# Two kinds of projection in pairs of units: 512 weight columns per matmul

## The reference

```python
def parallel_mixer(h, ...):
    proj = h @ w_in
    lx, ly, fq, fk, fv, ff, rq, rk, rv, rg = jnp.split(proj, ...)   # 256 256 512 512 512 8 256 256 256 256
    lru_out = rg_lru(causal_depthwise_conv(lx, ...), ...) * jax.nn.gelu(ly)
    fox_out = forgetting_attention(fq, fk, fv, ff, fox_b_f)         # 8 heads of 64
    ret_out = retention(rq, rk, rv, rg, positions)                  # 4 heads of 64, rotary on rq and rk
    return jnp.concatenate([lru_out, fox_out, ret_out], axis=-1) @ w_out

def memory_cross_attention(h, mem_n, w_q, w_k, w_v, w_o):
    ...
    v = (mem_n @ w_v).reshape(bsz, m, CROSS_HEADS, CROSS_HEAD_DIM)
    ...
```

## Time and profile before

| | us |
|---|---|
| median of 3 runs | 2244.64 (2243.01 to 2245.59) |
| profiled execution | 2244.02 |
| its span | 2242.2 |
| PE busy | 1789.8 (80%) |
| DVE busy | 842.8 (38%) |
| ACT busy | 551.4 (25%) |

### The profile page before, as it was taken

How to read it: one execution, slowest core, us unless ns; L and a number is a source line. 1 busy time by engine, 2 the same in 40 slices (tenths; PEclk the granted TensorE clock), 3 DMA queues, 4 the chain that set the end, 5 groups by cost and what they waited for, 6 DMA issues and landing times.

```text
span 2242.2 us, 27619 instructions
## 1 busy us (share of the span) xinstructions
PE 1789.8 (80%) x11942; PEld 1119.9 (50%) x11942; DVE 842.8 (38%) x1328; ACT 551.4 (25%) x841; POOL 88.0 (4%) x136
## 2 busy tenths in 40 slices
PE   8999999999999999998666666665666666576666
PEld 7899888899888888864112111221111211121111
DVE  5755788867678887741100100110010010010101
ACT  5745544456545444630000000000000000000000
POOL 1200000012100000000000000000000000000000
PEclk9999999999999999999878877887887887888788
DMA  8345667754547675599999999999999999999997
GB/s 265 130 157 194 196 226 250 239 172 143 197 150 234 228 262 168 226 426 429 430 429 430 429 430 429 429 430 430 428 430 429 430 430 430 430 429 430 429 430 315
DMA packets 172217, 739.73 MB, mean 330 GB/s; under 512 B 6800, under 2 KB 133264, under 8 KB 147008
## 3 DMA queue, kind: packets, MB, share of 16 engines
q1 hardware_dynamic: 169744, 731.27, 81.8%
q0 software_dynamic: 2352, 6.69, 0.9%
HBM read 736.88 MB, written 1.05 MB: 329 GB/s over the span
## 4 chain that ended last, share of the span: by engine, by line
DMA 49%; PE 41%; DVE 5%; ACT 2%; issue 1%; POOL 0%; SPq 0%; DVEq 0%; POOLq 0%; ACTq 0%
PE PS L399 40%; DMA WB<-in_w_up 24%; DMA WB<-in_w_down 24%; DVE WL L1853 1%; DMA W<-in_w_in 1%; ACT WH L1278 1%; DVE S L1848 1%; DVE X L1848 1%; PE PS L558 0%; POOL T L2742 0%; DVE CN L1845 0%; DVE S L1845 0%; PE PS L687 0%; DVE S L1962 0%; PE PS L532 0%
## 5 line engine op out<-in xcount | busy, mean ns | idle before, releaser
L399 PE MATMUL PS<-WB,XS 128*32 128x352 f32 x3520 | 405.7, 621 | 238.5 <-DMA WB<-in_w_up 163.1
L399 PE MATMUL PS<-HT,WH 128*128 128x256 f32 (+1 forms) x1456 | 383.9, 338 | 4.7 <-DVE WL L1853 2.4
L399 PEld LDWEIGHTS PS<-WB,XS 128*32 128x32 f32 x3520 | 130.2, 138 | 508.4 <-DMA WB<-in_w_up 218.7
L1853 DVE TENSOR_TENSOR WL<-W,WH 128x2048 fp32r<-128x2048 f32 x135 | 310.2, 2298 | 132.6 <-ACT WH L1278 132.5
L1278 ACT ACTIVATE WH<-W 128x2048 fp32r<-128x2048 f32 x141 | 270.0, 1915 | 244.4 <-PE PS L399 242.2
L399 PE MATMUL PS<-WB,S 128*32 128x512 f32 x1054 | 221.8, 773 | 118.5 <-DMA WB<-in_w_down 92.3
L1848 DVE SCALAR_TENSOR_TENSOR S<-S,PS 128x352 f32<-128x352 f32 (+1 forms) x66 | 33.3, 525 | 717.6 <-PE PS L399 402.4
L399 PE MATMUL PS<-HT,WL 128*128 128x256 f32 x1064 | 296.7, 282 | 0.0
L399 PEld LDWEIGHTS PS<-HT,WH 128*128 128x128 f32 x1456 | 249.7, 191 | 36.7 <-DVE WL L1853 3.6
L399 PE MATMUL PS<-WH,MX 128*128 128x512 f32 x672 | 216.2, 394 | 1.3 <-DVE MX L2333 0.9
L399 PEld LDWEIGHTS PS<-HT,WL 128*128 128x128 f32 x1064 | 203.3, 191 | 0.8
(11 more groups left out here) (281 smaller groups left out, 1879.1 us busy)
## 6 DMA issues: line engine op xcount, KB each, us to landing
WB<-in_w_up SPq DMA_DIRECT2D x63, 2816.0 KB, 36.3
WB<-in_w_gate SPq DMA_DIRECT2D x47, 2816.0 KB, 35.2
WB<-in_w_down SPq DMA_DIRECT2D x46, 2816.0 KB, 35.9
CN<-in_w_gate SPq DMA_DIRECT2D x16, 2816.0 KB, 36.5
CN<-in_w_down SPq DMA_DIRECT2D x15, 2816.0 KB, 36.1
W<-in_w_in SPq DMA_DIRECT2D x31, 1024.0 KB, 5.4
S<-in_w_ada SPq DMA_DIRECT2D x24, 1024.0 KB, 5.3
W<-in_w_gate SPq DMA_DIRECT2D x22, 1024.0 KB, 7.8
```

The source lines that it names most:

```text
L399: return e.matmul(o, l, r, start=start, stop=stop, skip_group_check=True)
L1853: e.tensor_tensor(M.WL[i][:, :], M.SLOT[m % NW], M.WH[i][:, :].bitcast(F32), ALU.subtract).then_inc(*up("low", m))
```

## The change

The units of v, of rq with rk, and of rv with rg in the mixer, and those of w_cv, no longer hold 256 columns of all 1024 rows. A unit is now 512 columns of 512 rows (`wide`), and two such units make a pair that adds up in two whole PSUM banks, one for each half of the tokens. The first of a pair takes both banks and keeps them (`Banks.take_pair`), the second releases them. The tokens stand and 512 columns move. The order of units in the mixer becomes v, v, q, k, and rq with rk, rv with rg; the copies out of PSUM move behind the second unit of a pair. The gate's tanh reads half of each bank of the rv and rg pair, and so does DVE's product with it.

```diff
     def begin(self):
         self.next, self.held, self.n = 0, {}, [0] * 4
...
+    def take_pair(self, name):
+        b = (0, 2, 2, 0)[self.next]
+        if {b, b + 1} & set(self.held.values()):
+            b = 2 - b
+        assert not {b, b + 1} & set(self.held.values()), name
+        for t in range(2):
+            self.n[b + t] += 1
+            self.uses[(*name, t)] = (b + t, self.n[b + t])
+            self.held[(*name, t)] = b + t
+        self.next = (b + 2) % 4
...
+    def wide(name, l, col, src, to, half):
+
+        m, u = unit(name, l, "wide", col, half)
+        if not half:
+            C.banks.take_pair(to)
+        for t in range(2):
+            i, k = C.banks.uses[(*to, t)]
+            if not half and k > 1:
+                e.wait_ge(C.sig.sem(f"bank{i}"), k - 1)
+            for k in range(4):
+                ins = mm3(PS[:, 4 + i, :], part(src, slice(None), 4 * half + k, slice(128 * t, 128 * t + 128)),
+                          part(u, slice(None), k), half == k == 0, half == 1 and k == 3)
+            if t:
+                ins.then_inc(*up("unit", m))
+            beside.step()
+        if half:
+            drop((*to, 0))
+            drop((*to, 1))
+            same(("full", *to), ("unit", m))
...
-            proj_r("w_cv", l, n, MEM, ("v", l, n))
+            wide("w_cv", l, 512 * (n // 2), MEM, ("v", l, n // 2), n % 2)
...
-        proj_r("w_in", l, 6, HT, ("vv", l, 0))
+        wide("w_in", l, 1536, HT, ("vv", l), 0)
...
         heads(0)
+        wide("w_in", l, 1536, HT, ("vv", l), 1)
+        heads(1)
         proj_t("w_in", l, 3, HT, ("q", l, 1))
-        heads(1)
+        heads(2)
         proj_t("w_in", l, 5, HT, ("kk", l, 1))
-        heads(2)
-        proj_r("w_in", l, 7, HT, ("vv", l, 1))
         heads(3)
-        proj_r("w_in", l, 8, HT, ("rq", l), off=8)
+        wide("w_in", l, 2056, HT, ("rqk", l), 0)
         heads(4)
-        proj_r("w_in", l, 9, HT, ("rk", l), off=8)
+        wide("w_in", l, 2056, HT, ("rqk", l), 1)
         heads(5)
-        proj_r("w_in", l, 10, HT, ("rv", l), off=8)
+        wide("w_in", l, 2568, HT, ("rvg", l), 0)
         heads(6)
-        proj_r("w_in", l, 11, HT, ("rg", l), off=8)
+        wide("w_in", l, 2568, HT, ("rvg", l), 1)
         heads(7)
...
-        e.activation(M.S1, two(full("rq", l)), ACT.Copy).then_inc(*freed("rq", l))
         unit(heads, 4)
-        e.activation(M.QR, two(full("rk", l)), ACT.Copy).then_inc(*freed("rk", l))
+        ps = full_pair("rqk", l)
+        for t in range(2):
+            e.activation(M.RAW[:, :, t, :], two(ps[:, t, :]), ACT.Copy).then_inc(*freed("rqk", l, t))
         unit(heads, 5)
-        e.activation(M.RV, two(full("rv", l)), ACT.Copy).then_inc(*freed("rv", l))
         unit(heads, 6)
-        ps = two(full("rg", l))
-        e.wait_ge(*at("rot", l, 0, 1))
-        e.activation(M.S1, ps, ACT.Tanh, scale=0.5).then_inc(*up("rg_tanh", l))
+        ps = full_pair("rvg", l)
+        e.activation(M.S1, ps[:, :, 256:512], ACT.Tanh, scale=0.5).then_inc(*up("rg_tanh", l))
+        e.activation(M.RV, ps[:, :, 0:256], ACT.Copy).then_inc(*up("rg_tanh", l, "rv"))
...
+        elif kind == "wide":
+            src, a = w[512 * off:512 * off + 512, n:n + 512], 4
```

More of the change, by code:

```diff
@@ L123, in take @@
             i = (i + 1) % 4
-        self.next = i + 1
+        self.next = (i + 1) % 4
         self.n[i] += 1
@@ L409, in unit @@
         e.wait_ge(*(at("low", m, "half") if halves else at("low", m)))
-        a = 8 if kind == "cols" else 2
+        a = {"cols": 8, "wide": 4, "rows": 2}[kind]
         return m, [x[i][:, :].rearrange("p (a b) -> p a b", a=a) for x in (M.WH, M.WL)]
@@ L697, in values @@
             e.wait_ge(*at("pt_out", l, 2 * c + 1))
-            if c % 2 == 0:
-                e.wait_ge(*free("vv", l, c // 2))
+            if c == 0:
+                for t in range(2):
+                    e.wait_ge(*free("vv", l, t))
             for m, (a, b, q) in enumerate(((0, 256, 0), (128, 256, 256))):
@@ L731, in ret_v @@
             if h == 0:
-                e.wait_ge(*free("rv", l))
+                e.wait_ge(*at("rg_tanh", l, "rv"))
             v0, v1 = (M.RV[:, t, 64 * h:64 * h + 64] for t in range(2))
@@ L830, in values @@
             if h == 0:
-                for n in range(4):
-                    e.wait_ge(*free("v", l, n))
+                for n in range(2):
+                    for t in range(2):
+                        e.wait_ge(*free("v", l, n, t))
             for d in range(2):
@@ L1302, in full, with full_pair @@
         return PS[:, 4 + i, :]
+    def full_pair(*use):
+        e.wait_ge(*at("full", *use))
+        i, _ = C.banks.uses[(*use, 0)]
+        return PS[:, 4 + i:6 + i, :]
     def squares(name, src, ready, tiles=(0, 1)):
@@ L1365, in fill_out @@
             e.activation(M.CK[:, 2 * n:2 * n + 2, :], two(full("k", l, n)), ACT.Copy).then_inc(*freed("k", l, n))
-        else:
-            e.activation(M.CV[:, :, 256 * n:256 * n + 256], two(full("v", l, n)), ACT.Copy).then_inc(*freed("v", l, n))
+        elif n % 2:
+            n //= 2
+            ps = full_pair("v", l, n)
+            for t in range(2):
+                e.activation(M.CV[:, t, 512 * n:512 * n + 512], ps[:, t, :], ACT.Copy).then_inc(*freed("v", l, n, t))
     def norm_after(place, nrm, layer):
@@ L1464, in k_out, with v_out @@
             e.activation(M.KT[:, 2 * n:2 * n + 2, :], two(full("kk", l, n)), ACT.Copy).then_inc(*freed("kk", l, n))
-        def v_out(n):
-            e.activation(M.V[:, :, 256 * n:256 * n + 256], two(full("vv", l, n)), ACT.Copy).then_inc(*freed("vv", l, n))
+        def v_out():
+            ps = full_pair("vv", l)
+            for t in range(2):
+                e.activation(M.V[:, t, :], ps[:, t, :], ACT.Copy).then_inc(*freed("vv", l, t))
         unit()
@@ L1482, in mixer @@
         unit()
-        v_out(0)
         beside.finish(fg)
@@ L1522, in mixer @@
         unit(heads, 0)
+        v_out()
+        unit(heads, 1)
         q_out(1)
-        unit(heads, 1)
+        unit(heads, 2)
         k_out(1)
-        unit(heads, 2)
-        v_out(1)
         unit(heads, 3)
@@ L2276, in retained @@
             own()
-            e.wait_ge(*free("rg", l))
+            for t in range(2):
+                e.wait_ge(*free("rvg", l, t))
             stt(flat(M.A3), flat(M.A3), 0.5, flat(M.RG), ALU.mult, ALU.mult).then_inc(*up("gated", l))
@@ L2286, in mixer @@
             next(turns, None)
-        ps = two(full("rg", l))
-        e.wait_ge(*at("rg_tanh", l))
-        stt(flat(M.RG), flat(M.S1), 1.0, flat(ps), ALU.add, ALU.mult).then_inc(*freed("rg", l))
+        e.wait_ge(*at("full", "rvg", l))
+        e.wait_ge(*at("rg_tanh", l, "rv"))
+        for t in range(2):
+            i, _ = C.banks.uses[("rvg", l, t)]
+            stt(M.RG[:, t, :], M.S1[:, t, :], 1.0, PS[:, 4 + i, 256:512], ALU.add, ALU.mult).then_inc(*freed("rvg", l, t))
         if l == 0:
@@ L2777, in gpsimd_program @@
         e.wait_ge(*at("forget", l))
-        for n, (raw, res) in enumerate(((M.S1, M.RQ), (M.QR, M.RK))):
+        for t in range(2):
+            e.wait_ge(*free("rqk", l, t))
+        for n, (raw, res) in enumerate(((M.RAW[:, 0], M.RQ), (M.RAW[:, 1], M.RK))):
             x, o = (v.rearrange("p t (h s f) -> p t h s f", h=4, s=2) for v in (raw, res))
-            e.wait_ge(*free("rk" if n else "rq", l))
             for s in range(2):
@@ L2840, in load_unit @@
         w, a = D[name][l], 8
-        src = w[:, 256 * n + off:256 * n + off + 256] if kind == "cols" else w[256 * n:256 * n + 256, :]
-        if kind == "rows":
-            a = 2
+        if kind == "cols":
+            src = w[:, 256 * n + off:256 * n + off + 256]
+        elif kind == "wide":
+            src, a = w[512 * off:512 * off + 512, n:n + 512], 4
+        else:
+            src, a = w[256 * n:256 * n + 256, :], 2
         if m >= NW:
@@ L2896, in buffer @@
             lo, hi = M.PLACE[i]
-            e.wait_ge(*at("full", "v", 1, 3))
+            e.wait_ge(*at("full", "v", 1, 1))
             e.wait_ge(*at("full", "ug", 1))
```

1 line of the change is left out of this document (added).

## The result

The changed kernel takes 2248.97 us (median of 13 runs, 2247.76 to 2250.1) against 2244.62 for the kernel before (13 runs). The ratio is 1.002, interval 1.0013 to 1.0027: 4.4 us slower, where 4.0 us faster was forecast and 2236 to 2246.5 was the range.

A forecast was written before the change was run, and what follows sets the result against it. Bound: PE in the dense half, then expert weight loads at a fixed rate, so dense gains reach the end. Sum: -6.4 + 0.5 + 0.3 + 0.4 + 1.2 = -4.0 us, giving 2240.6 us; range 2236 to 2246.5.

The forecast's parts named there:

- a wait not seen here: Anywhere: with five slow stretches, one of two ways to a slower result, above 2249.1 us; 6% together.
- The wide matmul: Ten pairs in mixers and w_cv: 512 columns at 0.2267 us against 256 at 0.120, saving 6.4 us.
- rival of a smaller win per matmul (b): Edited units: the wide matmul wins less, giving 2243.6 or 2245.4 us; 10% together.
- Waits in layer 0: Mixer of layer 0: new 2.3 us wait before the rv pair, one grows 0.14, two go; net +0.3 us.
- those of 0.63 and 1.50: Layer 0's attention heads: two existing PE waits of 0.63 and 1.50 us, both claimed to go.
- a race between two chains: Before layer 0's rv pair: copy of rq and rk 1.7 us earlier, PE 1.13 earlier; wait 2.2 to 2.3 us.
- Clock: Behind layer 0's new wait: a 1.2 GHz stretch costing 1.6 to 2.5 us, replacing the old 1.64; +0.4 us.
- Layer 1: Retention scores after the second w_cv unit wait for both ACT copies of that pair: +1.2 us.
- a relief of DVE in layer 0: Layer 0's heads: POOL's rotary starts after the pair's copy, so DVE's split and scalings are 1.2 us faster.
- Hidden beside the norm: Norm after layer 1's mixer: the 1.75 us wait grows to about 2.1; together 0.5 us of gain lost.
- Rival (c): Clock falls after more waits, 1.64 us a stretch; 17% for one or two, 8% for more.
- five stretches: Slow-clock stretches, 1.64 us each: five, or an unseen wait, needed to pass 2249.1 us; 6%.
- Rival (d): Layer 0's mixer: ACT and DVE set its heads, six units lose their 0.32, -2.1 and 2242.5 us; 10%.

The follow-up runs named there:

- e1: Changed kernel with the last two key units before layer 0's FFN back in PSUM banks 3 and 0: 2242.69 us, ratio to the kernel before 0.9992.
- e2: Kernel before, with the same two key units moved from banks 3 and 0 to 2 and 3: 2251.32 us, ratio 1.0029.
- e5: As e4, with layer 0's four pairs of turned memory two units later, beside the units of rv and rg: 2243.13 us.
- e6: As e5, but the turned memory only one unit later (4 steps of padding in place of 6): 2242.77 us.
- e4: As e1, with layer 1's retention scores of the first two heads in banks 0 and 1, not 2 and 3: 2240.91 us, ratio 0.9983.
- e8: As e4, but in layer 1 GpSimd turns only one of four heads of rq and rk: 2241.86 us.
- the four orders of layer 0's heads: Four runs moving ScalarE's copy of rq and rk, the turned memory, or both, against e1 or e4: 2243.22, 2243.13, 2242.77 and 2241.87 us.

## Why the prediction was wrong

**The step that failed** is the place where it looked for waits. It followed the banks through the two mixers and to the scores behind them and took "a wait not seen here" as part of the 6% left for slower. It never followed the counter to the next place with a fixed bank, the FFN of layer 0, some 80 us behind the last w_cv unit of that layer and some 155 behind the last edited unit of its mixer. By e1 that place costs 6.3 us, by e2 7.1. With it the forecast of -4.0 becomes +2.3 to +3.1. Two smaller misses, told below, add the wait of 0.8 us in layer 1 and about 1.2 us of gain that layer 0's mixer does not pass on: +4.3 to +5.1. Measured was +4.4.

**Of the terms of the sum:**

- The wide matmul: 0.2267 us as taken. The rival of a smaller win per matmul (b) is out.
- Waits in layer 0: 2.54 for 2.3, 1.00 for 0.74; those of 0.63 and 1.50 gone as said. The mechanism was right, and e5 shows it apart. The working was not: it put the wait down to a race between two chains, but both begin at one copy (e6), and that is why the wait is 2.54 in all profiles that have it. That its 2.3 came so near is in part luck.
- Clock: taken as 2.0 us behind the new wait. Seven profiles have this wait of 2.54; the unit behind it took 8.43, 5.62, 8.12, 8.10, 7.05, 7.26 and 7.02 us, so the tail was 0 to 2.8, 1.8 in the mean. In e2 the old wait of 1.50 had no tail either: the unit took 5.92 us, where the earlier trace rows has 7.40. The old tail was thus 1.5 us, a little less than the 1.64 taken against 48 x 0.120. The size was fair as a mean; one trace could not give it.
- Layer 1: the wait at the scores 1.22 for 1.2, and e4 gives 1.8 back. What was missed is 0.76 us at the last probabilities: the prediction used POOL's later start as a relief of DVE in layer 0 and did not ask which work it runs beside instead. e8 shows that.
- Hidden beside the norm: that wait is 1.66, not the 2.1 foreseen. Before, ACT copied a w_cv unit (589.24, 0.60 us) ahead of the weight split that leads to the norm; now that copy stands behind the second unit of the pair, and the norm comes 0.55 us earlier, counted from the start of the w_cv unit before the last (19.48 us before, 18.93 now). The prediction let PE come earlier and the norm stay.
- Rival (c), more slow stretches: one came, behind a wait that (c) had not listed. By (c)'s own price five stretches give 2248.8 us, short of the 2249.1 that they were to pass.
- Rival (d), that the gain does not reach the end of layer 0's mixer, held in the main. e1 has the wide mixer and e2 the old one, and neither has a slow stretch there. From the first v unit to the first w_cv unit e1 takes 117.21 us and e2 117.58 (rows below). So 0.4 us arrive of the 1.6 forecast, six units of 0.32 less the 0.3 of waits. PE of e1 is 1.3 us ahead at the first w_ck unit, but then it waits 0.73 us for DVE, whose split and scalings one head earlier took 2.86 and 1.32 us beside POOL, as in layer 1. That this is the reason is read from two profiles; no run tests it. In the mixer of layer 1 the lead does grow unit by unit, 0.3 us each.

PE of e1, then PE of e2:

```profile
41.33 0.50 PE L411 MATMUL PS<-WH,HT 128*128 128x512 f32 x1 [0.54 <-DVE WL L1901]
...
111.88 0.52 PE L724 MATMUL PS<-CN 128*128 128x128 f32 x3 [0.73 <-DVE CN L1893]
...
158.54 0.39 PE L411 MATMUL PS<-WH,MEMh 128*128 128x512 f32 x1
```
```profile
41.95 0.39 PE L399 MATMUL PS<-WH,HT 128*128 128x256 f32 x1 [0.54 <-DVE WL L1858]
...
159.53 0.28 PE L399 MATMUL PS<-WH,MEMh 128*128 128x256 f32 x1
```

**What stays unexplained.** e1 less before is -1.6 us; -4.0 plus the 0.8 of layer 1 and the 1.2 of layer 0's mixer is -2.0. The 0.4 us between are far less than the interval of e1's ratio is wide (4 us), and the clock's tail alone varies by more. The profiles of before and after also differ by 1.6 us at the program's start, ahead of all edited units (26.92 and 28.49 us). The first such point, the first matmul of the forget gate, stands between 26.4 and 28.5 us in the twelve profiles, in no order that follows the edits; I take it as scatter, without a test. So of the 6.1 us between the two profiles, 4.5 are left beside the 4.4 between the medians.

## What to carry to other kernels

Where buffers are handed out by a counter, an edit that takes them in other sizes moves every later use that the counter hands out. List the waits of all later users before and after, to the end of the program, above all those that name a fixed buffer. A buffer's price is the place of its copy in the copying engine's queue, not the length of the copy. And where two helper engines are already behind, as the four orders of layer 0's heads suggest, reordering moves a wait from place to place. That less work there would remove it is not tested.

## What the runs showed of the hardware

The same wait of PE, before the same matmuls, was followed by a half-clock stretch in some profiles and by none in others: 0 to 2.8 us for the wait of 2.54, 0 or 1.5 for that of 1.50. The tail of the 4.95 us wait was about 2 us in the changed kernel and less, 1.4, in e2 (7.22 us for the unit). The Trainium skill, page "TensorE: Matmul & The Clock Gate", section "What's actually happening", says that the number of slow matmuls at a kernel's start differs from run to run of the same kernel; these traces show the like in the middle of kernels that have the same instructions there. A price for the clock should be a range from none to the largest seen.
